# Sample attention with the probabilities held still in four column tiles, and its loads issued from two engines

## The reference, cut to what matters

```python
# B = 8 sequences, Lq = 4 new tokens, 2 groups x 4 heads, head width 64, past of 512 tokens
past = cache_nsa_kv[l][page_table].reshape(8, 512, 4, 2, 64)    # four pages of 128 tokens each
...
p_cmp = gqa_probs(q, k_cmp, ...); o_cmp = gqa_apply(p_cmp, v_cmp)     # 31 compressed keys
o_sel = sel_attend(q, idx, q_pos, ksb, vsb, table_g)                  # past + new rows, all blocks
wkv = jnp.concatenate([win_buf, kv_new[:, :, 4:]], axis=1)
o_win = gqa_apply(gqa_probs(q, wkv[:, :, 0], mask, ...), wkv[:, :, 1])  # window of 512 + new rows
o = gates[..., 0] * o_cmp + gates[..., 1] * o_sel + gates[..., 2] * o_win
```

## Time and profile before

| what | value |
|---|---|
| median of three runs | 3393.26 us (3388.26 to 3394.25) |
| the profiled execution's own time | 3394.81 us |
| its span, first to last instruction | 3393.0 us |
| mean granted TensorE clock | 0.927 of full speed |
| TensorE busy | 3085.4 us, 91% of the span |
| VectorE, ScalarE busy | 1357.9 us, 964.5 us |

### The profile page before, as it was taken

How to read it: one execution, slowest core, us unless ns; L and a number is a source line. 1 busy time by engine, 2 the same in 40 slices (tenths; PEclk the granted TensorE clock), 3 DMA queues, 4 the chain that set the end, 5 groups by cost and what they waited for, 6 DMA issues and landing times. The chain is left out here.

```text
span 3393.0 us, 58789 instructions
## 1 busy us (share of the span) xinstructions
PE 3085.4 (91%) x24907; PEld 2919.5 (86%) x24907; DVE 1357.9 (40%) x2813; ACT 964.5 (28%) x1594; POOL 55.4 (2%) x32
## 2 busy tenths in 40 slices
PE   6999998699679998999989999878987899899997
PEld 4999998578469998999989999867865898899997
DVE  4232344256236354333342333433541735533334
ACT  2222222244133143222232222322430513322222
POOL 0000000000011000000000000000000300000000
PEclk7999998799769898999999999889986889899998
DMA  6645334232333245333256422443122525233321
GB/s 216 227 155 171 89 83 146 71 112 57 106 100 86 79 136 174 121 89 88 80 173 202 150 88 85 129 126 99 54 57 69 142 63 156 69 88 88 88 88 64
DMA packets 523702, 378.64 MB, mean 112 GB/s; under 512 B 43058, under 2 KB 469448, under 8 KB 522131
## 3 DMA queue, kind: packets, MB, share of 16 engines
q1 hardware_dynamic: 486932, 307.17, 30.9%
q10 hardware_dynamic: 36512, 67.77, 5.7%
HBM read 344.10 MB, written 39.07 MB: 113 GB/s over the span
## 5 line engine op out<-in xcount | busy, mean ns | idle before, releaser
L192 DVE TENSOR_TENSOR w_lo<-w_raw,w_hi 128x1024 fp32r<-128x1024 f32 (+1 forms) x390 | 481.3, 1234 | 1125.8 <-ACT w_hi L187 1125.7
L187 ACT ACTIVATE w_hi<-w_raw 128x1024 fp32r<-128x1024 f32 (+1 forms) x390 | 405.7, 1041 | 1333.6 <-PE pa L204 680.9
L204 PE MATMUL pa<-nhi,w_hi 128*128 128x272 f32 x1408 | 296.7, 292 | 29.1 <-DVE nlo L247 27.3
L204 PE MATMUL pa<-nhi,w_lo 128*128 128x272 f32 x1408 | 293.2, 290 | 0.0
L204 PE MATMUL pg<-nhi,w_hi 128*128 128x272 f32 x1408 | 292.9, 289 | 0.0
L204 PE MATMUL pa<-ghi,w_hi 128*128 128x272 f32 x1408 | 291.6, 288 | 1.3 <-DVE glo L794 1.3
L204 PE MATMUL pg<-nhi,w_lo 128*128 128x272 f32 x1408 | 292.5, 289 | 0.0
L204 PE MATMUL pa<-nlo,w_hi 128*128 128x272 f32 x1408 | 292.4, 289 | 0.0
L204 PE MATMUL pg<-nlo,w_hi 128*128 128x272 f32 x1408 | 291.9, 289 | 0.0
L204 PE MATMUL pa<-ghi,w_lo 128*128 128x272 f32 x1408 | 291.0, 288 | 0.0
L204 PE MATMUL pa<-glo,w_hi 128*128 128x272 f32 x1408 | 290.4, 288 | 0.0
(11 more groups left out here) (340 smaller groups left out, 4750.7 us busy)
## 6 DMA issues: line engine op xcount, KB each, us to landing
w_raw<-in_ffn_w_in SPq DMA_DIRECT2D x352, 192.0 KB, 2.8
ada_raw<-in_ada_w ACTq DMA_DIRECT2D x26, 2048.0 KB, 10.0
w_raw<-in_w_in SPq DMA_DIRECT2D x156, 192.0 KB, 2.9
w_raw<-in_ffn_w_out SPq DMA_DIRECT2D x128, 192.0 KB, 2.7
w_raw<-in_ffn_w_in SPq DMA_DIRECT2D x176, 128.0 KB, 2.9
ada_raw<-in_ada_w SPq DMA_DIRECT2D x10, 2048.0 KB, 15.6
w_raw<-in_ffn_w_out SPq DMA_DIRECT2D x160, 128.0 KB, 2.4
w_raw<-in_w_in SPq DMA_DIRECT2D x94, 128.0 KB, 3.1
```

Source lines behind the costliest of these rows:

```text
L187: act.activation(self.hi[slot][:, 0:k, :], self.raw[slot][:, 0:k, :], ACT.Copy).then_inc(self.hi_done, 1)
L192: dve.tensor_tensor(self.lo[slot][:, 0:k, :], self.raw[slot][:, 0:k, :], self.hi[slot][:, 0:k, :].bitcast(F32), ALU.subtract).then_inc(sel ...
L204: mm = pe.matmul(out[:, half, 0:HALF], w[slot][:, k0 + n, :], x[:, n, half * HALF:(half + 1) * HALF], start=(n == 0 and w is self.hi and x ...
```

## The change

1. In the values' products the operands trade places: 32 columns of `pT` (one sequence's queries) are held still in one of four column tiles, and the 128 value columns move. Four sequences `j` follow each other for the same `br` and `t`. The result has queries on the partitions.
2. So a half's result is copied to SBUF by VectorE (`save`, into space of `kT`), transposed by TensorE (`turn_output`) and copied to `oa` in two pieces instead of eight (`outputs`).
3. The transposing of the first half's probabilities, `turn(0)`, moves ahead of `turn_keys(7)`, its copies ahead of the copies of the keys of sequence 7, and `values(0)` follows the scores of sequence 7 directly.
4. ScalarE issues the loads of sequences 1 and 3 at the start of the stage, of 5 after its key copy of sequence 0, and of 7 after that of sequence 1. SyncE issues those of 0, 2, 4 and 6.

```diff
@@ sync
-                    for b in range(NB):
+                    for b in range(0, NB, 2):
                         load_sequence(sp, l, b, kv[b // 4], rows_in[b])
...
@@ tensor
+                    def values(half):
+                        pe.wait_ge(ta_done, half + 1)
+                        pe.wait_ge(tb_done, half + 1)
+                        out = po[half][:, 0, 0:P]
+                        rows = [slice(32 * j, 32 * j + 32) for j in range(4)]
+                        pe.matmul(out, pT[0:NSMP, 0, 4, :], kvn[0:NSMP, 4, 3 * P:4 * P], start=True, stop=False)
+                        for j in range(4):
+                            pe.matmul(out[rows[j], :], pTc[0:NCMP, rows[j]], vcn[0:NCMP, 4 * half + j, :], start=False, stop=False)
+                        for br in range(2):
+                            for t in range(4):
+                                for j in range(4):
+                                    pe.matmul(out[rows[j], :], pT[:, br, t, rows[j]], kv[half][:, j, br, t, P:2 * P],
+                                              start=False, stop=False)
+                        pe.matmul(out, pT[0:NSMP, 1, 4, :], kvn[0:NSMP, 4, 5 * P:6 * P], start=False,
+                                  stop=True).then_inc(pv_done, 1)
+                    def turn_output(half):
+                        pe.wait_ge(ob_done, half + 1)
+                        pe.transpose(po[half][:, 0, P:2 * P], ov[:, half, :], ident[:, :]).then_inc(ot_done, 1)
...
                             if b + 1 < NB:
+                                if b + 1 == NB - 1:
+                                    turn(0)
+                                    pe.wait_ge(ta_done, 1)
+                                    pe.wait_ge(tb_done, 1)
                                 turn_keys(b + 1)
...
-                    for half in range(2):
-                        pe.wait_ge(p_done, 3 * (half + 1))
...
-                            for br in range(2):
-                                for t in range(4):
-                                    pe.matmul(out, kv[half][:, j, br, t, P:2 * P], pT[:, br, t, cols], start=False, stop=False)
...
+                    values(0)
+                    turn(1)
+                    turn_output(0)
+                    values(1)
+                    turn_output(1)
@@ vector
+                            if b == NB - 1:
+                                copy_turned(0)
                             dve.wait_ge(kt_done, b + 1)
...
+                    def save(half):
+                        dve.wait_ge(pv_done, half + 1)
+                        dve.tensor_copy(ov[:, half, :], po[half][:, 0, 0:P]).then_inc(ob_done, 1)
...
+                            dve.tensor_copy(strided(oa[rows, 0, SEQ + 16 * half:], [T, R], [NI, 4], [1, NI]),
+                                            strided(po[half][rows, 0, P + 16 * g:], [NI, R], [32, 4], [1, NI]))
...
                     weigh(1)
-                    copy_turned(0)
-                    outputs(0)
-                    copy_turned(1)
-                    outputs(1)
+                    save(0)
+                    copy_turned(1)
+                    outputs(0)
+                    save(1)
+                    outputs(1)
@@ scalar
+                    load_sequence(act, l, 1, kv[0], rows_in[1])
+                    load_sequence(act, l, 3, kv[0], rows_in[3])
                     for half in range(2):
                         for j in range(4):
                             b = 4 * half + j
+                            if b == NB - 1:
+                                copy_turned(0)
                             act.wait_ge(kt_done, b + 1)
...
                             act.activation(kT[:, b % 2, 0, :], pk[0][:, 0, :], ACT.Copy).then_inc(ka_done, 1)
+                            if b < 2:
+                                load_sequence(act, l, 5 + 2 * b, kv[1], rows_in[5 + 2 * b])
```

More of the change, by code:

```diff
@@ L1403, in sample_stage @@
                        "s_done", "sa_done", "mx_done", "neg_done", "exp_done", "w_done", "p_done", "t_done", "ta_done",
-                       "tb_done", "pv_done", "sq_done") as (
+                       "tb_done", "pv_done", "sq_done", "ob_done", "ot_done") as (
                     in0, in1, in2, in3, in4, in5, in6, in7, gs_in, qbd_done, kt_done, ka_done, kb_done, s_done, sa_done, mx_done,
-                    neg_done, exp_done, w_done, p_done, t_done, ta_done, tb_done, pv_done, sq_done), ExitStack() as st:
+                    neg_done, exp_done, w_done, p_done, t_done, ta_done, tb_done, pv_done, sq_done, ob_done,
+                    ot_done), ExitStack() as st:
                 rows_in = [in0, in1, in2, in3, in4, in5, in6, in7]
@@ L1414, in sample_stage @@
                 pTc = sb("pTc", [32, P], at=st)
+                ov = kT[:, 0, 0, 0:2 * P].rearrange("p (h q) -> p h q", h=2)
                 mx = sb("mx", [P, 2, 5], at=st)
@@ L1447, in turn_keys, with turn @@
                         mm.then_inc(kt_done, 1)
+                    def turn(half):
+                        pe.wait_ge(p_done, 3 * (half + 1))
+                        if half:
+                            pe.wait_ge(ta_done, 1)
+                            pe.wait_ge(tb_done, 1)
+                        for br in range(2):
+                            for t in range(4):
+                                pe.transpose(pk[br][:, 0, t * P:(t + 1) * P], sc[half][:, br, t * P:(t + 1) * P], ident[:, :])
+                        for br in range(2):
+                            pe.transpose(ptn[0:NSMP, 0, br * P:(br + 1) * P], sc[half][:, br, PAST:PAST + NSMP], ident[:, :])
+                        pe.transpose(ptn[0:NCMP, 0, 2 * P:3 * P], scc[:, half, 0:NCMP], ident[:, :]).then_inc(t_done, 1)
+                    def values(half):
[6 more added lines that the diff above has]
+                            pe.matmul(out[rows[j], :], pTc[0:NCMP, rows[j]], vcn[0:NCMP, 4 * half + j, :], start=False, stop=False)
+                        for br in range(2):
+                            for t in range(4):
+                                for j in range(4):
[6 more added lines that the diff above has]
+                        pe.transpose(po[half][:, 0, P:2 * P], ov[:, half, :], ident[:, :]).then_inc(ot_done, 1)
                     turn_keys(0)
@@ L1469, in _ @@
                             mm.then_inc(s_done, 1)
-                    for half in range(2):
-                        pe.wait_ge(p_done, 3 * (half + 1))
-                        if half:
-                            pe.wait_ge(ta_done, 1)
-                            pe.wait_ge(tb_done, 1)
-                        for br in range(2):
-                            for t in range(4):
[L1477 to L1492, removed]
-                                    pe.matmul(out, kv[half][:, j, br, t, P:2 * P], pT[:, br, t, cols], start=False, stop=False)
-                        pe.matmul(po[half][:, 0, 0:P], kvn[0:NSMP, 4, 5 * P:6 * P], pT[0:NSMP, 1, 4, :], start=False,
-                                  stop=True).then_inc(pv_done, 1)
+                    values(0)
[3 more added lines that the diff above has]
+                    turn_output(1)
                 @block.vector
@@ L1545, in copy_turned @@
                         dve.tensor_copy(pT[:, 1, 0:4, :], pk[1][:, 0, :].rearrange("p (t q) -> p t q", t=4)).then_inc(tb_done, 1)
+                    def save(half):
+                        dve.wait_ge(pv_done, half + 1)
+                        dve.tensor_copy(ov[:, half, :], po[half][:, 0, 0:P]).then_inc(ob_done, 1)
                     def outputs(half):
-                        dve.wait_ge(pv_done, half + 1)
+                        dve.wait_ge(ot_done, half + 1)
                         for g in range(GROUPS):
                             rows = slice(g * DH, (g + 1) * DH)
[L1551 to L1554, removed]
+                            dve.tensor_copy(strided(oa[rows, 0, SEQ + 16 * half:], [T, R], [NI, 4], [1, NI]),
+                                            strided(po[half][rows, 0, P + 16 * g:], [NI, R], [32, 4], [1, NI]))
                     maxima(0)
@@ L1566, in _, with copy_turned @@
                 def _(act):
+                    def copy_turned(half):
+                        act.wait_ge(t_done, half + 1)
+                        if half:
+                            act.wait_ge(pv_done, 1)
+                        act.activation(pT[:, 0, 0:4, :], pk[0][:, 0, :].rearrange("p (t q) -> p t q", t=4), ACT.Copy).then_inc(ta_done, 1)
+                    load_sequence(act, l, 1, kv[0], rows_in[1])
+                    load_sequence(act, l, 3, kv[0], rows_in[3])
                     for half in range(2):
```

## The result

The changed kernel takes 3317.32 us (median of four runs, 3310.98 to 3319.61) against 3393.76 us before: a ratio of 0.9774 with a 95% interval of 0.9757 to 0.9792. That is 76.4 us off; the forecast was 3325 us, 68 off. In the profiled executions, 3394.81 and 3310.98 us, the mean granted clock rose from 0.927 to 0.941; the second of them is the fastest of its four.

The account below looks back on a forecast made before the run. TensorE (91% busy) was taken to bound the kernel, the sample stage by load issue, softmax and value products in turn. Gains of 65.3 and 3.4 us off 3394.81 gave 3326.1, with the median's 1.55 offset 3325; range 3314 to 3346.

Parts of the forecast that it names:

- The values and the tail: Sample stage, second half's first maximum to last copy: 14.45 us against 47.10, a gain of 32.65 us a layer.
- values of a half: Value products of one half of the sequences: 3.2 to 5.0 us, middle 4.1, in place of 17.6.
- ScalarE's issue: Start of the sample stage: each load takes ScalarE 6.19 us, as SyncE; its key copies queue behind and hold TensorE back.
- The time up to T8: First load issue to second half's first maximum: 59.6 us against 61.67 and 61.86, called a gain of 1.7 a layer.
- T8: The first maximum of the second half's softmax, forecast 59.6 us after the first load issue.
- the 35.8: First load issue to the first half's first maximum, in us: 26.6 + 5.5 + 3.0 + 0.7, against 36.77 before.
- the 17.3: Keys of sequence 5 to T8, in us: 18.4 less 3.91 of load waits, plus `turn(0)` and its copies; up to 18.5.
- The sum: Whole kernel: 65.3 us from the tails and 3.4 up to T8, 68.7 off the profiled 3394.81.
- Dearer issue on ScalarE: Rival on the split loads: ScalarE's issue costs more than SyncE's, delaying key copies; 3335 to 3352 us, chance 0.13.
- Cheaper issue: Rival on the split loads: ScalarE issues a load in 5 us, 4.8 us earlier a layer; 3315 us, chance 0.06.
- Tiles without overlap: Rival on the value products: each record pays load and matmul in full, 29 us a half; 3420 us, chance 0.02.
- The new products do what they say: Denies a rival on the value products: tiles take turns, only loads are hidden, 11 us a half; 3349 us, chance 0.04.

Follow-up runs that it names:

- loads alone: The kernel before with ScalarE issuing the loads of the odd sequences, old order of work and old products kept: 3375.74 us, ratio 0.9951.
- old operands: The changed kernel with the old products (values held still, 32 columns move) and no transposing of the output: 3361.22 us, ratio 0.9905.
- tile after tile: The changed kernel with the loop over the four column tiles outermost, eight products of one tile in a row: 3324.90 us, ratio 0.9798.
- filler: The changed kernel with the first half's 32 tile products made once more into columns that nothing reads: 3309.18 us, ratio 0.9747.
- late-issue: The changed kernel with ScalarE issuing loads 1 and 3 first, 7 after its copy of sequence 3, SyncE the others: 3312.12 us, ratio 0.9754.

## Why the prediction was right, and where it was short

- **The values and the tail: right.** 14.45 us forecast, 14.09 and 14.08 measured; a gain of 66.0 us for 65.3. The terms: `turn(1)` 2.61 us (taken as 2.0), copies to `pT` 1.39 with the handover (1.4), values of a half 3.1 (4.1), the last transposes and copies 1.2 (1.32). So the sum is closer than its terms: 0.6 too little for `turn(1)`, at the lower clock, offset most of the 1.0 too much for the values. The softmax covers `values(0)` as argued. The row of line 419 was the right one to price the products by: the new ones take 1.95 us for 64 records too. One reading there was wrong, though: its slower burst did not open a stretch; TensorE had been busy for 7.10 of 7.10 us before it (49.20 to 56.30), at a granted clock of 0.50. The two times stand, the reason given for them does not. And what this rests on is shown: with the turns of the four tiles taken away, the products cost three times as much. The rule of the Trainium skill ("TensorE: Matmul & The Clock Gate", Part 3) that a weight load overlaps running matmuls only where row groups differ does not agree with these runs: all four column tiles share their row groups, and the records stand 30 ns apart with loads of 110 ns.
- **ScalarE's issue: right.** 6.03 us for the first load, taken as 6.19; the copies of 1 and 2 stand behind the loads and TensorE waits for them. The copy of sequence 2 ends 26.7 us after the first issue (26.6 forecast), 25.5 in the second layer. Within that, two errors offset each other. The first keys started 11.8 and 11.1 us after the first issue, 2.5 and 1.6 later than before (up to 1 was allowed): with two queues issuing, the first load lands later, for with SyncE alone in the same kernel it was 8.5 and 8.2. And a load between two copies took ScalarE 5.3 to 5.8 us in place of 6.19.
- **The time up to T8: the right mechanism, mis-sized.** The step that failed is "T8 = 35.8 + 6.5 + 17.3 = 59.6", called a gain of 1.7 a layer. (Two slips stand in that working: 59.6 lies 2.1 and 2.3 below the old T8, not 1.7, and two dense pairs bound the 35.8 at 33.3, not 32.3.) Measured: 35.0 + 6.4 + 14.9 = 56.3 and 32.2 + 6.4 + 14.6 = 53.2, gains of 5.4 and 8.7, both beyond the stated bound of 4.4. In the 17.3 I took the waits out of the 18.4 us and left the work as it was, but the work depends on the clock that it meets.
  - From keys 7 to T8 it takes 4.59 us in both layers (923.82 to 928.41) where I left 6.04. There the lower clock went with the wait: keys 7 ran at a granted clock of 0.50 behind 2.45 us of waiting, and run at 1.00 now. The kernel with the loads alone has 4.62 us here, without any wait.
  - Keys 5 and scores 4 take 4.61 us (913.52 to 918.13) where I counted 5.5. Here no wait went away; the one before them is 6.46 us for 6.54. The price varies by itself: the kernel before has 5.5 us in the first layer and 4.55, less its wait for a load, in the second, the kernel with the loads alone 4.31 and 5.48, at granted clocks from 0.50 to 0.65. I had read one layer. These are the rows of the kernel before in its second layer:

```profile
2571.10 1.94 PE L1446 MATMUL pk<-ident,kv 128*128 128x128 f32 x8 [6.45 <-DVE kT L1511]
...
2576.21 1.07 PE L1446 MATMUL pk<-ident,kv 128*128 128x128 f32 x8 [0.56 <-DMA kv<-in_state_win_kv]
```

  - From keys 3 to the first half's maximum it takes 8.26 us in the first layer (898.84 to 907.10) and 6.62 in the second (2508.71 to 2515.33, all at 1.00), for 9.2, though TensorE had waited 3.37 and 2.96 us for ScalarE. Of the second layer's 8.7 us, 6.6 lie in this first half.
  - In the kernel with the loads alone the second half falls by 6.5 us in the first layer. Of these 3.91 were waits, 1.4 are the clock behind the last wait, and 1.2 are the varying price of keys 5 and scores 4. So part of the size was luck.
- **The sum.** 68.7 us were forecast between profiled executions, and the stages gave 80.0: 0.7 more in the tails, 10.6 more up to T8.
- **The rivals.** Dearer issue on ScalarE: no, 6.03 us. Cheaper issue: half so, 5.3 to 5.8 us for the loads between copies. The time of 3317 lies nearer to that rival's 3315 than to 3325, but not for its reason: it would have the copy of sequence 2 done at 21.8 us, and that came at 26.7 and 25.5. Tiles without overlap: no. The new products do what they say.

Open: the first half of the same code (changed, loads alone, old operands, tile after tile, filler) spreads from 32.2 to 37.0 us. Its rows differ in when a load lands and in which pairs of keys and scores meet the upper clock. I have not separated the two, nor what moves the landings.

## What to carry to other kernels

Price a product by its instruction form: hold the small operand still in column tiles, let the wide one move, and let consecutive products go to different tiles. When a wait is taken away, ask also at which clock the work behind it ran: it can get faster too, as from keys 7 to T8, but not every wait is followed by the lower clock, and a price read from one layer can be off by a fifth. And an engine that issues loads is busy while it does so: put its issues where nothing in its queue is waited for.

## What the runs showed of the hardware

- A TensorE that is busy without a gap can lose its upper clock: products with 128 loaded and 32 moved columns went from 0.97 to 0.50 after 2.8 us, and stayed there for the 12.7 us that followed. With 32 loaded and 128 moved, bursts of 1.95 us (in turns) and 5.96 us (tile after tile) that began at 1.00 stayed there; one that began at 0.50, in the late-issue kernel, ran at 0.50 for 3.64 us.
- 64 records of products in four column tiles take 1.95 us in turns and 5.96 tile after tile, with the same loads of 110 ns and at the same clock.
- Useless products in an idle stretch shortened the tail by 1.2 us, in four tails of four.
- Two issuing queues moved 240 GB/s at a DMA share of 0.98, one 147 at 0.49: the share doubled for 1.6 times the data, so what each transfer occupies grew too, and the first keys started 2.9 to 3.3 us later than with one queue in the same kernel.
